# Eight of twelve adaLN parts moved from TensorE to VectorE, as row sums over transposed weight pieces that sit in three of the weight ring's slots

## The chip, the cores and the metric

The kernel runs on one core of one Trainium2 chip. The metric is the device time of one execution, in microseconds (us). Before the change it is 1217.66 us (median of three runs, 1216.58 to 1221.11).

## The reference

Two groups of 128 tokens, a context group and a latent group (256 token columns in all, width 1024), go through two layers of the same form. Each layer first computes a modulation from a condition vector: one fixed vector for the context group, one given vector for the latent group.

```python
mod = silu(cond) @ w_ada + b_ada          # w_ada is 1024 x 6144, per layer
sh1, sc1, g1, sh2, sc2, g2 = split(mod, 6)
h = rms_norm(x, norm1) * (1 + sc1) + sh1
# attention, Hyena and retention branches from h @ w_in, gates from h @ w_gate
x = x + g1 * (merged @ w_out)
h2 = rms_norm(x, norm2) * (1 + sc2) + sh2
x = x + g2 * moe(h2, ...)
```

All is float32. The six parts of `mod` have 1024 values for each of the two condition vectors. Each needs 4 MB of `w_ada`. Two layers of six parts make the twelve parts of the title. A part is named here by layer and number: (0, 2) is `g1` of layer 0; numbers 0 to 5 are sh1, sc1, g1, sh2, sc2, g2.

## The kernel before

**Weights.** SyncE's queue (line 541) fetches all weights in pieces of 1 MB in an order fixed beforehand (`weight_plan`, `ring_table`). The pieces go into a ring of eight slots (`ring`); for the experts six more slots (`lent`) join, once the last merge piece is used. A fetch waits until TensorE has counted off the piece that was in its slot before (`s_weights_used`). The queue is in order: a fetch that waits holds up all fetches behind it.

**A layer, dense half.** TensorE works through units. Units 0 to 29 (`proj`, L747 and L752) are 32 matmuls of 256 columns over one 1 MB piece each. Unit u writes PSUM bank u % 4, and takes it only when the reader of unit u - 4 has freed it. Units 0 to 5 are Hyena's: ScalarE makes the middle tap (L1415), VectorE adds the two other taps and frees the bank (L1660). Behind unit 2, ScalarE and VectorE also make the decay tables of the retention (`decay_tables`, L1394 to L1408 on ScalarE, L1652 to L1660 on VectorE). Units 6 and up are queries, keys, values, gates. Small products stand between the units: Fourier products (L815), retention scores, the eight softmaxes of the attention at units 19 to 27 (scores L891 and L892). Then come six merge pieces (L932) and four output pieces (L961). Each engine's order is written out by hand; engines meet only at semaphores.

**Opening of layer 0** (`first_units_of_first`): units 0 to 3 go in two halves of the depth, with Hyena's filter products (L714 to L728) and part (0, 1) in between.

**The modulation.** All twelve parts are made alike. `ada` (L676) takes four 1 MB pieces and issues 64 matmuls, the condition `condT` as the stationary operand. ScalarE copies the result to `mod_row` (`mod_rows`, L1323), `ada_turn` transposes it with two matmuls (L688), and VectorE adds the bias and makes the factors (`mod_add`). Where each part stands in the order is given by `ADA_AFTER`: (0, 2), (0, 3), (0, 4) behind units 4, 5, 7 of layer 0; (1, 1) and (1, 0) in the merge of layer 0; (1, 2) ahead of unit 0 of layer 1, and (1, 3), (1, 4) behind its units 3 and 5. (0, 0) and (0, 1) stand in the opening, (0, 5) and (1, 5) between the router and the experts.

**Experts half.** 96 pieces of 1 MB per layer, each used once (L1056, L1095, L1071, L1113), with gathers (L1036) and combines (L1136) of tokens in between.

**GpSimd's queue** issues the small loads and stores; in layer 0 the caches are loaded after part (0, 1) is there, and in layer 1 after the last expert piece of layer 0 is used.

Of the kernel before, what the change touches and what calls it, by code (L numbers as in the profile page):

```python
# [17 lines left out]
ALU = mybir.AluOpType  # L18
# [63 lines left out]
def ada_bank(layer, u):  # L82

    return {(0, 5): 5, (0, 7): 7}.get((layer, u), 4)
# [9 lines left out]
def weight_plan():  # L94

    plan = []
    for layer in range(DEPTH):
        if layer == 0:
            plan += OPENING
        for u in range(0 if layer else 3, U_MERGE):  # L100
            beside = [("ada", layer, ADA_AFTER[layer, u])] if (layer, u) in ADA_AFTER else []
            plan += beside + [("proj", layer, u)] if u == 0 else [("proj", layer, u)] + beside
        for m in range(6):
            plan.append(("merge", layer, m))
            if m in (2, 4) and layer + 1 < DEPTH:
                plan.append(("ada", layer + 1, 1 if m == 2 else 0))
# [12 lines left out]
def ring_table():  # L119
# [19 lines left out]
SLOT, FILL, USED = ring_table()  # L139
ADA_ORDER = [item[1:] for item in PLAN if item[0] == "ada"]  # L140


def ada_at(layer, q):

    return ADA_ORDER.index((layer, q))

# [119 lines left out]
def trunk_program(nc, row_scratch, weights, experts, mod_params, params, consts, shared, x_in, k_cache, v_cache, s_cache,  # L266
                  y_out, k_out, v_out, s_out):
    with ExitStack() as ctx:
# [38 lines left out]
        s_b_half = sem("b_half")  # L307
# [7 lines left out]
        s_decay_log = sem("decay_log")  # L315
        s_decay_one = sem("decay_one")
# [12 lines left out]
        s_lam_sums = sem("lam_sums")  # L329
# [17 lines left out]
        s_mod_sum = sem("mod_sum")  # L347
        s_norm_mean = sem("norm_mean")
# [18 lines left out]
        s_scalar_link = sem("scalar_link")  # L367
# [5 lines left out]
        s_stores_read = sem("stores_read")  # L373
        s_taps = sem("taps")
        s_taps_abs = sem("taps_abs")
        s_taps_decayed = sem("taps_decayed")
# [35 lines left out]
        uc = sb("uc", P, 12, TOK)  # L412

# [116 lines left out]
        def _(sp):  # L530
            sp.dma_start(x[:, :, :], x_in).then_inc(s_x_in, 16)
            sp.dma_start(shd[:, :], shared).then_inc(s_shared_in, 16)
            n = dense = 0

# [9 lines left out]
            for kind, layer, _ in PLAN:  # L544
# [6 lines left out]
                sp.wait_ge(s_stores_read, layer + 1)  # L551
# [32 lines left out]
        def _(pool):  # L584
# [15 lines left out]
            for layer in range(DEPTH):  # L600
# [12 lines left out]
                pool.dma_start(sc[:, :, :, :], s_cache[layer]).then_inc(s_cache_in, 16)  # L613
                pool.wait_ge(s_qkr_copied, 2 * layer + 2)
# [16 lines left out]
                pool.sem_inc(s_stores_read, 1)  # L631
# [10 lines left out]
        def _(pe):  # L642
# [49 lines left out]
            def filter_step(layer, n):  # L692
# [30 lines left out]
                else:  # L723
                    pe.wait_ge(s_taps, layer + 1)
# [194 lines left out]
            def merge(layer):  # L919
                u = U_MERGE  # L920
                for half in range(2):
                    for branch, src, event in ((1, uc, s_yb_ready), (2, gr, s_yc_ready),
# [16 lines left out]
                        if (half, branch) == (1, 2):  # L939
                            turn_rows(layer)  # L940
                            if layer + 1 < DEPTH:
                                ada(layer + 1, 0, 4)
                        if layer + 1 < DEPTH and (half, branch) == (1, 0):
                            ada_turn(layer + 1, 0, 4)
                        if layer + 1 < DEPTH and (half, branch) == (0, 0):
                            ada(layer + 1, 1, 4)
                        if layer + 1 < DEPTH and (half, branch) == (1, 1):
                            ada_turn(layer + 1, 1, 4)
# [234 lines left out]
            for layer in range(DEPTH):  # L1183
# [7 lines left out]
                else:  # L1191
                    ada(layer, ADA_AFTER[layer, 0], 4)
                    first_units(layer)
                for u in range(U_MERGE):
                    if u >= (2 if layer else 4):
                        proj(layer, u)
                    if u and (layer, u) in ADA_AFTER:
# [1261 lines left out]
```

## Time and profile before

| | us |
|---|---|
| median of three runs | 1217.66 |
| profiled execution, its own time | 1220.16 |
| span of that execution (first to last instruction) | 1218.4 |
| TensorE matmuls busy in the span | 1171.0 (96%) |
| TensorE weight loads busy | 897.5 (74%) |
| VectorE busy | 359.9 (30%) |
| ScalarE busy | 216.3 (18%) |
| mean granted TensorE clock | 0.986 of full |

All later readings are in us from the start of the span. Layer 0 runs from 0 to about 632, layer 1 from there to the end; in each the experts start about 250 us before its end. The chain of waits is the path followed back from the last instruction. A row of the timeline gives start, duration, engine, line, and in brackets how long the engine sat idle before it and what it waited for. "PEclk" is the granted TensorE clock as a share of full speed (1.00 is 2.4 GHz, 0.50 is 1.2 GHz).

### The profile page before, as it was taken

How to read it: one execution, taken by the hardware profiler on the slowest of the kernel's cores; microseconds unless marked ns; L12 is line 12 of the kernel's file. 1: busy time of each engine (PE TensorE's matmuls, PEld its weight loads, DVE VectorE, ACT ScalarE, POOL GpSimd, SP SyncE). 2: the span in 40 equal slices, each digit the busy share in tenths (PEclk: the TensorE clock that was granted, in tenths of full speed). 3: DMA queues.
4: the chain of work that ended last, by engine and by line, in shares of the span. 5: the costliest groups of instructions: out<-in, count | busy, mean ns of one | idle time of the engine just before them, and what ended most of it. 6: DMA issues, size and time to landing. Idle time of an engine off the chain costs nothing.

```text
span 1218.4 us, 18282 instructions
## 1 busy us (share of the span) xinstructions
PE 1171.0 (96%) x7494; PEld 897.5 (74%) x7494; DVE 359.9 (30%) x905; ACT 216.3 (18%) x459; POOL 39.5 (3%) x80
## 2 busy tenths in 40 slices
PE   6999999999999999989999999999999999998996
PEld 4778888878788775646558888888888877565653
DVE  2541153133326321111233323332242541111113
ACT  2140012232011100111024111132301201000011
POOL 1001110000000000000000012000000000000000
PEclk8999999999998999999999999999999899999998
DMA  9879534333797998999986945343247599899992
GB/s 383 339 284 393 183 130 142 136 112 139 278 408 306 405 401 341 421 421 420 421 331 258 373 153 165 113 147 138 107 155 314 231 391 416 326 423 420 421 420 109
DMA packets 50874, 349.46 MB, mean 287 GB/s; under 512 B 6401, under 2 KB 6561, under 8 KB 9569
## 3 DMA queue, kind: packets, MB, share of 16 engines
q1 hardware_dynamic: 46944, 337.75, 69.7%
q0 software_dynamic: 3840, 10.47, 2.5%
q8 instruction: 62, 1.02, 0.3%
q14 instruction: 28, 0.22, 0.1%
HBM read 343.98 MB, written 2.64 MB: 284 GB/s over the span
## 4 chain that ended last, share of the span: by engine, by line
PE 87%; DMA 8%; DVE 2%; ACT 1%; SPq 1%; issue 1%; DVEq 0%; ACTq 0%
PE bank L752 25%; PE bank L1056 12%; PE bank L1095 7%; PE bank L932 7%; PE bank L961 5%; PE bank L747 5%; PE bank L1036 4%; DMA ring<-in_experts 4%; PE bank L763 4%; PE bank L1136 4%; PE bank L676 4%; DMA lent<-in_experts 3%; DMA ring<-in_weights 1%; PE bank L1071 1%; PE bank L1012 1%; SPq L541 1%
## 5 line engine op out<-in xcount | busy, mean ns | idle before, releaser
L752 PE MATMUL bank<-h,ring 128*128 128x256 f32 x1472 | 326.3, 380 | 0.0
L752 PEld LDWEIGHTS bank<-h,ring 128*128 128x128 f32 x1472 | 276.8, 190 | 40.9 <-issue 4.4
L1056 PE MATMUL bank<-ring,gates 128*64 128x256 f32 (+2 forms) x1280 | 148.7, 379 | 7.1 <-DMA lent<-in_experts 3.5
L1056 PEld LDWEIGHTS bank<-ring,gates 128*64 128x64 f32 (+2 forms) x1280 | 104.3, 137 | 45.4 <-issue 7.5
L1095 PE MATMUL bank<-lent,gates 128*64 128x512 f32 (+2 forms) x288 | 67.0, 637 | 9.5 <-DMA lent<-in_experts 9.5
L1056 PE MATMUL bank<-lent,gates 128*64 128x256 f32 (+1 forms) x640 | 64.7, 380 | 1.4 <-ACT gates L1580 1.4
L1036 PE MATMUL bank<-uc,gates 128*128 128x128 f32 x512 | 60.4, 276 | 0.1
L1036 PEld LDWEIGHTS bank<-uc,gates 128*128 128x128 f32 x512 | 58.6, 192 | 0.7 <-DVE uc L1656 0.4
L932 PE MATMUL bank<-lent,ring 128*128 128x256 f32 x256 | 56.4, 380 | 0.0
L747 PE MATMUL bank<-ring,h 128*128 128x256 f32 x256 | 56.4, 379 | 0.0
L961 PE MATMUL bank<-uc,ring 128*128 128x256 f32 x256 | 55.6, 379 | 0.0
L1056 PEld LDWEIGHTS bank<-lent,gates 128*64 128x64 f32 (+1 forms) x640 | 39.2, 126 | 21.2 <-issue 2.3
L1095 PEld LDWEIGHTS bank<-lent,gates 128*64 128x64 f32 (+2 forms) x288 | 21.3, 141 | 44.9 <-issue 44.9
L932 PEld LDWEIGHTS bank<-lent,ring 128*128 128x128 f32 x256 | 48.4, 190 | 6.9 <-issue 0.4
L961 PEld LDWEIGHTS bank<-uc,ring 128*128 128x128 f32 x256 | 48.6, 190 | 6.6
L1136 PEld LDWEIGHTS bank<-gates,uc 128*128 128x128 f32 x224 | 41.6, 190 | 15.8 <-issue 10.8
L747 PEld LDWEIGHTS bank<-ring,h 128*128 128x128 f32 x256 | 48.1, 190 | 6.2
L1660 DVE SCALAR_TENSOR_TENSOR gates<-gates,bank 128x512 f32<-128x512 f32 (+1 forms) x16 | 10.5, 654 | 141.3 <-issue 108.9
L1136 PE MATMUL bank<-gates,uc 128*128 128x256 f32 x224 | 51.9, 385 | 0.0
L763 PE MATMUL bank<-h,ring 128*128 128x256 f32 x192 | 46.2, 400 | 2.5 <-ACT h L1312 2.5
L2191 DVE COPY uc<-bank 128x512 f32<-128x512 f32 x14 | 9.7, 692 | 130.2 <-PE bank L1095 130.2
L1600 ACT ACTIVATE gates<-bank 128x512 f32<-128x512 f32 (+1 forms) x16 | 9.1, 570 | 212.2 <-PE bank L1056 190.3
(257 smaller groups left out, 1144.8 us busy)
## 6 DMA issues: line engine op xcount, KB each, us to landing
ring<-in_weights SPq DMA_DIRECT2D x128, 1024.0 KB, 5.7
ring<-in_experts SPq DMA_DIRECT2D x108, 1024.0 KB, 20.9
lent<-in_experts SPq DMA_DIRECT2D x84, 1024.0 KB, 16.7
lent<-lent POOLq DMA_DIRECT2D x48, 32.0 KB, 3.2
cst<-in_consts POOLq DMA_DIRECT2D x1, 1345.0 KB, 12.2
x<-in_x_in SPq DMA_DIRECT2D x1, 1024.0 KB, 4.9
lent<-in_s_cache POOLq DMA_DIRECT2D x2, 512.0 KB, 11.5
va<-row_scratch POOLq DMA_DIRECT2D x2, 512.0 KB, 6.7
```

The lines of the kernel that those rows point to most:

```text
L541: sp.dma_start(slot, source).then_inc(s_weights_in[SLOT[n]], 16)
L676: last = pe.matmul(bank[b][32 * j:32 * j + 32, 0:256], condT[:, k, :], w[j][:, k, :], start=(k == 0), stop=(k == KT - 1), skip_group_check ...
L747: last = pe.matmul(bank[b][:, g * 256:(g + 1) * 256], h[:, k, g_cols(g)], w[:, k, :], start=(k == 0), stop=(k == KT - 1))
L752: last = pe.matmul(bank[b][:, c * TOK:(c + 1) * TOK], w[:, k, c * P:(c + 1) * P], h[:, k, :], start=(k == 0), stop=(k == KT - 1))
L763: last = pe.matmul(bank[u][:, c * TOK:(c + 1) * TOK], w[:, k, c * P:(c + 1) * P], h[:, k, :], start=(k == 0 and c == 0), stop=(k == KT - 1 ...
L932: last = pe.matmul(bank[b][:, c * TOK:(c + 1) * TOK], w[:, k, d * P:(d + 1) * P], src[:, k, :], start=(k == 0), stop=(k == 3))
L961: last = pe.matmul(out[c], w[:, k, c * P:(c + 1) * P], merged[:, k, :], start=(k == 0), stop=(k == KT - 1))
L1012: last = pe.matmul(bank[b][:, c * P:(c + 1) * P], h[:, k, g_cols(n // 2)], ident, start=True, stop=True)
L1036: last = pe.matmul(bank[4 + half][:, c * P:(c + 1) * P], htok[:, g, k * P:(k + 1) * P], pick[p % 2][:, g, :], start=(g == 0), stop=(g == 1))
L1056: last = pe.matmul(bank[b][rows, half * 256:half * 256 + 256], hgat[:, k, rows], w[j][:, k, :], start=(k == 0), stop=(k == KT - 1), skip_g ...
L1095: last = pe.matmul(bank[5 - half][rows, :], actT[p % 2][:, f, rows], w[j][:, f, :], start=(f == 0), stop=(f == 3), skip_group_check=True)
L1136: last = pe.matmul(bank[dt // 2][:, (dt % 2) * TOK:(dt % 2 + 1) * TOK], ysb[:, dt * P:(dt + 1) * P], matrix, start=(fresh and dt % 2 == 0) ...
```

## The change

The eight parts (0, 2), (0, 3), (0, 4), (1, 0) to (1, 4) are no longer made by TensorE. `w_ada` for them is laid out transposed, in 64 chunks of 128 output columns by 1024 (512 KB), so that a row sum over a chunk times the condition gives 128 values of `mod`. VectorE does it with one scalar_tensor_tensor with a row sum for each of the two conditions. Parts (0, 0), (0, 1), (0, 5) and (1, 5) stay as they were.

Slots 5, 6 and 7 of the ring hold, through the dense half, the condition rows on all partitions (8 KB each), three landing places for chunks, and a dump for the product. So the dense pieces behind the opening use five slots (`LEAST`), and the experts eight and six as before. The condition rows are loaded raw by GpSimd's queue, once TensorE has used the opening's pieces up to unit 2; ScalarE takes a tanh behind its work on unit 1, VectorE makes the SiLU behind the decay tables, and the rows are stored to memory and loaded again for layer 1. Chunks are fetched by SyncE's queue, each behind a given piece of the plan; VectorE uses them at given places of its order (`HOOKS`, with the count of chunks at each in `AT_HOOK`).

```diff
-ADA_AFTER = {(0, 4): 2, (0, 5): 3, (0, 7): 4, (1, 0): 2, (1, 3): 3, (1, 5): 4}
+LEAST = 5
+MADE = [[(0, 2), (0, 3), (0, 4), (1, 0), (1, 1)], [(1, 2), (1, 3), (1, 4)]]
+CHUNKS = [8 * len(parts) for parts in MADE]
+LANDINGS = 3
+HOOKS = [("conv", 3, 3), ("conv", 4, 4), ("conv", 5, 5), ("rope", 0, 6), ("spectrum", 0, 9),
+         ("decay", 0, 10), ("spectrum", 1, 12), ("hyena", 1, 14), ("gate", 0, 16), ("retain", 1, 17),
+         ("softmax", 0, 18), ("softmax", 1, 19), ("softmax", 2, 20), ("softmax", 3, 21),
+         ("softmax", 4, 22), ("softmax", 5, 24), ("softmax", 7, 26), ("norm", 3, 28),
+         ("merge", 1, 30), ("merge", 3, 32), ("merge", 5, 34), ("merge", 7, 36), ("merge", 9, 38)]
+AT_HOOK = [[1, 1, 1, 6, 1, 3, 5, 1, 1, 2, 1, 1, 1, 1, 4, 1, 1, 4, 1, 1, 1, 1, 0],
+           [1, 1, 1, 5, 1, 3, 4, 1, 1, 2, 0, 1, 1, 1, 1, 0, 0, 0, 0, 0, 0, 0, 0]]
+def chunks_behind():
...
+            for c in range(count):
+                at = unit + 2 + c // LANDINGS
+                item = ("proj", layer, at) if at < U_MERGE else ("merge", layer, (at - U_MERGE) // 2)
+                behind.setdefault(item, []).append(n)
+                n += 1
...
-        since = {at: free[at] for at in range(SLOTS)}
+        own = SLOTS if kind == "moe" or (kind, layer, _) in OPENING else LEAST
+        since = {at: free[at] for at in range(own)}
...
+        cond_wide = ring[:, LEAST, :].rearrange("p (c k) -> p c k", c=2)
+        landing = [ring[:, LEAST + 1 + n // 2, D * (n % 2):D * (n % 2) + D] for n in range(LANDINGS)]
+        raw = ring[:, LEAST + 1, :]
+        product = ring[:, SLOTS - 1, D:2 * D]
...
+            def fetch_chunk():
+                nonlocal chunk
+                n = chunk % LANDINGS
+                if chunk == 0:
+                    sp.wait_ge(s_cond_ready, 2)
+                elif chunk == CHUNKS[0]:
+                    sp.wait_ge(s_weights_used, END["moe", 0, 0])
+                if chunk >= LANDINGS:
+                    sp.wait_ge(s_chunk_used, chunk - LANDINGS + 1)
+                sp.dma_start(landing[n], mod_weights[chunk, :, :]).then_inc(s_chunk_in[n], 16)
+                chunk += 1
...
                         fetch(weights[dense, :, :])
                         dense += 1
+                    for _ in CHUNKS_BEHIND.get((kind, layer, number), ()):
+                        fetch_chunk()
                     continue
...
+                sp.wait_ge(s_chunk_used, sum(CHUNKS[:layer + 1]))
...
                 if layer == 0:
+                    pool.wait_ge(s_weights_used, END["ada", 0, 1])
+                    pool.wait_ge(s_weights_used, MADE_FREE)
+                    pool.dma_start(raw, cond_rows.broadcast_to([P, 2 * D])).then_inc(s_cond_moved, 16)
                     pool.wait_ge(s_mod_ready, ada_at(0, 1) + 1)
...
                     pool.wait_ge(s_weights_used, END["moe", layer - 1, 0])
+                    pool.dma_start(flat(cond_wide), cond_scratch.broadcast_to([P, 2 * D])).then_inc(
+                        s_cond_moved, 16)
...
-                    ada(layer, ADA_AFTER[layer, 0], 4)
...
-                    if (layer, u) in ADA_AFTER:
-                        mod_rows(layer, ADA_AFTER[layer, u], ada_bank(layer, u))
+                    if layer == 0 and u == 1:
+                        sc_e.wait_ge(s_cond_moved, 16)
+                        sc_e.activation(flat(cond_wide), raw, ACT.Tanh, scale=0.5).then_inc(
+                            s_cond_tanh, 1)
...
+            def make_parts(layer, hook, number):
...
+                        dve.wait_ge(s_chunk_in[n % LANDINGS], 16 * (n // LANDINGS + 1))
...
+                        if n:
+                            dve.wait_ge(s_chunk_used, n)
+                        w = landing[n % LANDINGS]
+                        for c, out in enumerate((product, w)):
+                            last = dve.scalar_tensor_tensor(
+                                out, w, 0.5, cond_wide[:, c, :], ALU.mult, ALU.mult,
+                                accum_out=mod_all[:, of, row, c:c + 1])
+                        last.then_inc(s_chunk_used, 1)
+                        if n % 8 == 7:
+                            dve.wait_ge(s_chunk_used, n + 1)
+                            part_finish(of, q)
...
                     if u == 2:
                         decay_tables()
+                        if layer == 0:
+                            dve.wait_ge(s_cond_tanh, 2)
+                            stt(flat(cond_wide), flat(cond_wide), 1.0, raw, ALU.add, ALU.mult).then_inc(
+                                s_cond_ready, 1)
+                            dve.wait_ge(s_cond_ready, 2)
+                    make_parts(layer, "conv", u)
```

`MADE_FREE` is the count of `s_weights_used` at the end of unit 2 of layer 0. The calls of `ada`, `ada_turn`, `mod_rows` and `mod_add` for the eight parts are gone everywhere, also in the merge of layer 0. `part_finish` adds the bias and makes the factors (one or two small VectorE instructions per part). Calls of `make_parts` stand at the places that `HOOKS` names: ahead of a rotary step, a spectrum, a decay or a softmax, and behind a merge half-unit. A few semaphores that counted one event each are joined into one, with the same waits; ScalarE's waits on stores now read the stores' own semaphore.

## Rows read from the trace of the kernel before

**Rows 1.** The page, part 1: busy us, share of the span, instructions.

```profile
PE 1171.0 (96%) x7494; PEld 897.5 (74%) x7494; DVE 359.9 (30%) x905; ACT 216.3 (18%) x459; POOL 39.5 (3%) x80
```

**Rows 2.** Waits of TensorE, whole span: us in total, times, longest.

```profile
PE bank L1095 <- DMA lent<-in_experts: 9.5, 2, 4.9
```

**Rows 3.** The chain in order of time: start us, us, what.

```profile
69.82 6.91 PE bank L752 x32
76.72 3.59 PE bank L676 x64
...
683.38 3.59 PE bank L676 x64
```

**Rows 4.** Timeline of layer 0, a transpose between two units.

```profile
98.12 0.38 PE L688 MATMUL bank<-cst,rinv 128*128 128x128 f32 x2
...
98.34 7.07 PE L752 MATMUL bank<-h,ring 128*128 128x256 f32 x32
```

**Rows 5.** Timeline, start of layer 1.

```profile
633.00 3.66 PE L676 MATMUL bank<-ring,condT 128*32 128x256 f32 x64 [0.67 <-DVEq L1666]
...
635.75 0.49 ACT L1312 ACTIVATE h<-h,modT,amp 128x128 f32<-128x128 f32 x1 [2.35 <-DVE h L1652]
...
636.59 14.08 PE L763 MATMUL bank<-h,ring 128*128 128x256 f32 x64
...
651.57 13.98 PE L752 MATMUL bank<-h,ring 128*128 128x256 f32 x64
```

**Rows 6.** Windows of the opening: us, PE, PEld, DVE, ACT, POOL busy, PEclk, DMA share, GB/s.

```profile
21.60:25.10 3.50, 0.41 (x3) 0.23 (x3) 1.92 (x8) 0.88 (x2) 0.00 (x0) 0.88 1.02 421
25.10:28.50 3.40, 3.40 (x8) 2.74 (x9) 1.71 (x5) 2.76 (x4) 0.00 (x0) 0.50 1.00 419
28.50:31.70 3.20, 3.20 (x10) 2.27 (x9) 0.00 (x0) 0.00 (x0) 0.00 (x0) 0.60 1.02 424
```

**Rows 7.** Timeline of layer 0, units 2 and 3 and the decay tables.

```profile
62.75 7.07 PE L763 MATMUL bank<-h,ring 128*128 128x256 f32 x32
...
66.40 1.02 ACT L1415 ACTIVATE uc<-bank,par 128x256 f32<-128x256 f32 x2 [7.58 <-PE bank L763]
...
79.19 0.69 DVE L1652 TENSOR_TENSOR dsum<-dsum,lent 128x512 f32<-128x512 f32 x1
```

**Rows 8.** DMA issues: KB each, median us from issue to landing.

```profile
ring<-in_weights SPq DMA_DIRECT2D x128, 1024.0 KB, 5.7
...
cst<-in_consts POOLq DMA_DIRECT2D x1, 1345.0 KB, 12.2
...
va<-row_scratch POOLq DMA_DIRECT2D x2, 512.0 KB, 6.7
```

**Rows 9.** ScalarE's groups by shape: busy us, mean ns, idle before.

```profile
L1478 ACT ACTIVATION_READ_ACCUMULATOR lent<-bank,sm 128x1 f32 x32 | 6.3, 197 | 0.0
...
L1334 ACT ACTIVATE vr<-va 128x1024 f32<-128x1024 f32 x2 | 2.1, 1057 | 9.4 <-DVEq L1718 9.3
```

**Rows 10.** VectorE's groups by shape, same columns.

```profile
L1660 DVE SCALAR_TENSOR_TENSOR lent<-rinv,lent 128x512 f32<-128x512 f32 x4 | 2.8, 692 | 0.6
...
L1652 DVE TENSOR_TENSOR uc<-uc 128x1024 f32<-128x1024 f32 x2 | 2.5, 1226 | 0.3
```

**Rows 11.** Timeline of VectorE in layer 0, first work of softmaxes 1 and 4.

```profile
217.40 0.62 DVE L1910 TENSOR_REDUCE sm<-bank 128x1 f32<-128x128 f32 x2 [4.65 <-PE bank L892]
...
248.08 0.89 DVE L1910 TENSOR_REDUCE sm<-bank 128x1 f32<-128x256 f32 x2 [12.40 <-PE bank L892]
```

**Rows 12.** Windows of the two dense halves, columns as in group 6.

```profile
90.00:341.00 251.00, 249.79 (x1392) 209.94 (x1385) 77.38 (x147) 44.75 (x101) 16.14 (x31) 1.00 0.53 195
674.00:840.00 166.00, 166.00 (x872) 140.90 (x871) 47.66 (x93) 29.30 (x63) 14.54 (x28) 1.00 0.50 179
```

**Rows 13.** Timeline of SyncE's queue: first fetches of expert pieces.

```profile
341.62 3.07 SPq L541 DMA_DIRECT2D lent<-in_experts  x6
```

**Rows 14.** A window of the experts half of layer 0, columns as in group 6.

```profile
460.00:473.00 13.00, 13.00 (x118) 7.03 (x118) 2.32 (x9) 0.60 (x1) 0.00 (x0) 1.00 0.76 303
```

More of the change, by code:

```diff
@@ L74 @@
 ADA_PIECES = 4
-ADA_AFTER = {(0, 4): 2, (0, 5): 3, (0, 7): 4, (1, 0): 2, (1, 3): 3, (1, 5): 4}
+LEAST = 5
[9 more added lines that the diff above has]
+           [1, 1, 1, 5, 1, 3, 4, 1, 1, 2, 0, 1, 1, 1, 1, 0, 0, 0, 0, 0, 0, 0, 0]]
+assert [sum(n) for n in AT_HOOK] == CHUNKS
+def chunks_behind():
+    behind = {}
+    for layer in range(DEPTH):
+        n = 0
+        for (_, _, unit), count in zip(HOOKS, AT_HOOK[layer]):
+            for c in range(count):
[3 more added lines that the diff above has]
+                n += 1
+    return behind
 OPENING = [("ada", 0, 0), ("proj", 0, 0), ("proj", 0, 1), ("proj", 0, 2), ("ada", 0, 1)]
 OPENING_DONE = [("ada", 0, 0), ("ada", 0, 1), ("proj", 0, 0), ("proj", 0, 1), ("proj", 0, 2)]
-def ada_bank(layer, u):
-    return {(0, 5): 5, (0, 7): 7}.get((layer, u), 4)
 def ada_parts(layer, q):
@@ L100, in weight_plan @@
         for u in range(0 if layer else 3, U_MERGE):
-            beside = [("ada", layer, ADA_AFTER[layer, u])] if (layer, u) in ADA_AFTER else []
-            plan += beside + [("proj", layer, u)] if u == 0 else [("proj", layer, u)] + beside
+            plan.append(("proj", layer, u))
         for m in range(6):
             plan.append(("merge", layer, m))
-            if m in (2, 4) and layer + 1 < DEPTH:
-                plan.append(("ada", layer + 1, 1 if m == 2 else 0))
         plan += [("out", layer, u) for u in range(U_OUT, N_PROJ)]
@@ L145, in ada_at, with made_at @@
     return ADA_ORDER.index((layer, q))
+def made_at(layer, q):
+    return [part for parts in MADE for part in parts].index((layer, q)) + 1
 def proj_end(layer, u):
@@ L347, in trunk_program @@
         s_mod_sum = sem("mod_sum")
+        s_chunk_in = [sem(f"chunk_in{n}") for n in range(LANDINGS)]
+        s_chunk_used = sem("chunk_used")
+        s_part_made = sem("part_made")
+        s_cond_moved = sem("cond_rows_in_out_in")
         s_norm_mean = sem("norm_mean")
@@ L542, in fetch @@
                 n += 1
-            for kind, layer, _ in PLAN:
+            for kind, layer, number in PLAN:
                 if kind != "moe":
@@ L1308, in norm_shift @@
                 else:
-                    sc_e.wait_ge(s_mod_ready, 1 + max(ada_at(layer, q) for q in range(2)))
+                    sc_e.wait_ge(s_part_made, made_at(layer, 1))
                 for k in tiles_:
@@ L1709, in mod_add @@
                 if q == 2:
-                    link(ts(modT[:, 16:24, :], modT[:, 16:24, :], 0.5, ALU.mult))
-                dve.sem_inc(s_mod_ready, 1)
+                    link(ts(mine, mine, 0.5, ALU.mult))
+                dve.sem_inc(s_part_made, 1)
+            def make_parts(layer, hook, number):
+                for (name, which, _), count in zip(HOOKS, AT_HOOK[layer]):
+                    if (name, which) != (hook, number):
+                        continue
+                    for _ in range(count):
+                        n = made[0]
+                        made[0] += 1
+                        of, q = MADE[layer][(n - sum(CHUNKS[:layer])) // 8]
+                        row = 8 * q + n % 8
+                        dve.wait_ge(s_chunk_in[n % LANDINGS], 16 * (n // LANDINGS + 1))
+                        if n == CHUNKS[0]:
+                            dve.wait_ge(s_cond_moved, 48)
+                        if n:
[9 more added lines that the diff above has]
+                            part_finish(of, q)
             def taps_decay(layer):
@@ L1930, in _ @@
                 dve.sem_inc(s_qx_ready, 1)
+                make_parts(layer, "spectrum", 0)
                 spectrum(0)
+                make_parts(layer, "decay", 0)
                 ret_decay(0)
+                make_parts(layer, "spectrum", 1)
                 spectrum(1)
@@ L1946, in _ @@
                         ret_decay(1)
+                make_parts(layer, "gate", 0)
                 yc_gate(0)
@@ L1958, in _ @@
                 for i in range(8):
+                    make_parts(layer, "softmax", i)
                     if i == 5:
@@ L1964, in _ @@
                         ya(0)
+                make_parts(layer, "norm", 3)
                 o_mean(3)
@@ L1996, in _ @@
                                 dve.sem_inc(s_merged, 1)
+                            make_parts(layer, "merge", u - U_MERGE)
                             u += 1
-                        if layer + 1 < DEPTH and (half, n) == (1, 0):
-                            mod_add(layer + 1, 1, 4)
-                        if layer + 1 < DEPTH and (half, n) == (1, 2):
-                            mod_add(layer + 1, 0, 4)
                 def square_add(t):
@@ L2383, in lay_out @@
     weights = np.stack(pieces)
+    mod_weights = np.stack([a["w_ada"][l][:, D * q + P * t:D * q + P * t + P].T
+                            for parts in MADE for l, q in parts for t in range(KT)])
+    cond_rows = np.concatenate([a["c_ctx"].reshape(-1), a["c"][0].reshape(-1)])[None]
     experts = np.stack([np.stack([
```

95 lines of the change are left out of this document (39 added, 56 removed).

## The prediction

> **What bounds the kernel now.** I read the shares first. TensorE is busy 96% of the span and VectorE 30% [rows 1]. So work that leaves TensorE is worth its time, where nothing else then ends last. The waits of TensorE say where that could be: its largest is for expert weights, 9.5 us in two waits [rows 2], so the experts half is nearly paced by DMA and the dense half is not. The chain agrees. In the dense half it is unit behind unit, 6.91 us each, and the parts stand in it in full, 3.59 us each; of those removed it holds seven at that length, from the one at 76.72 to the one at 683.38 [rows 3]. The chain shows no cover for them.
>
> **What goes.** Seven parts stand between other work: 7 x 3.59 = 25.1 us. Each has its transposes too: a unit ends at 98.12, the next starts at 98.34 [rows 4], 0.22 us, seven times 1.5 us. The eighth, (1, 2), runs at 633.00 while layer 1's norm is made. The first h tile is ready at 635.75 + 0.49 = 636.24 and units 0 and 1 start at 636.59, so removing it brings 0.35 us there. Their 64 matmuls last 2 x 6.91 = 13.8 us, to 650.4, and unit 2 starts at 651.57 [rows 5]: 1.1 us for that part's transposes and their wait for ScalarE's copy go as well. In all 25.1 + 1.5 + 1.5 = 28.1 us. Most of it lies in stages where every gap is full, so I take it whole; the least would be 25.1 alone.
>
> **The hole at the start of layer 1.** Without (1, 2) TensorE sits idle from the end of the norm's sum, 633.00 - 0.67 = 632.3 [rows 5], to about 636.3. The opening shows such a pause: 0.41 us of work in 3.5 us, and then the granted clock is 0.50 for 3.4 us and 0.60 on average for 3.2 us [rows 6]. That is 3.4 + 2.6 = 6.0 us at the lower of the two levels, 1.2 GHz, which loses half of it, 3.0 us. I take 3.0 us, from 0 (the clock holds) to 3.4.
>
> **The hole in layer 0, the largest cost.** Chunk 0 stands in SyncE's queue behind the piece of unit 5, and its fetch waits for the condition rows in their final form. The pieces of units 6 and up stand behind it; they were fetched freely before. Step by step:
> - Unit 2 is over at 66.3 (half of the row at 62.75) and ScalarE starts on it at 66.40 [rows 7]. Only then may GpSimd's queue load the raw rows, 1 MB on its software queue. The trace has 512 KB there in 6.7 us (a broadcast of the same kind) and 1345 KB in 12.2 us, the latter beside a full DMA; on SyncE's queue 1 MB takes 5.7 us [rows 8]. DMA is free at this point, since SyncE's queue waits, so I take 6.0 us: 72.4.
> - ScalarE waits for them behind unit 1's tap, ahead of unit 2's. Then the tanh over 2048 columns, twice the 1057 ns for 1024 [rows 9]: 2.1 us, to 74.5. So unit 2's tap, at 66.40 before, is 8.1 us late.
> - All that hangs on it moves by as much: the decay tables end at 79.19 + 0.69 = 79.9 before [rows 7], now at 88.0.
> - VectorE's SiLU over 2048 columns, twice 1226 ns [rows 10]: 90.4.
> - SyncE's queue issues chunk 0, then unit 6's piece (0.3 us), 5.7 us to land [rows 8], and half a megabyte is ahead of it, about 0.6 us at half of a landing's excess: 97.0.
> - TensorE does units 4 and 5 from 69.8, and would start unit 6 at 69.8 + 2 x 6.91 = 83.6. It waits until 97.0: 13.4 us. After such a hole I charge the low clock again, 3.0 us.
>
> The bounds: with the raw rows there at once, the decay tables still end at 79.9 and the piece lands at 88.9, a hole of 5.3 us and perhaps no loss of clock. With 12.2 us for the rows and 8.5 us for the piece it is 22.4 us and 3.0 for the clock. I take 16.4 us, from 5.3 to 25.4, near the middle because the uncontended rows are the nearest. The Trainium skill (DMA: Bandwidth & Descriptors, Anatomy of one DMA) fits a GpSimd DMA by a fixed 2.0 us plus its bytes at 436 GB/s, 4.4 us for this one by estimate; the sum would be 1.6 us lower by it. No row has a lone 1 MB on that queue.
>
> **What is added on VectorE.** A chunk is two instructions over 1024 columns. The trace has none with a row sum. The plain two-input instruction over 1024 takes 1226 ns, and scalar_tensor_tensor over two SBUF inputs takes the same as it at 512 columns, 692 ns [rows 10]. ScalarE's reading of a row sum is an instruction of its own, 197 ns [rows 9]. So a chunk is 2.45 us at least and 2.85 with that reading; I take 2.7, and 64 make 173 us. The other end is double, 4.9 us, a rival below. VectorE has 174 us of nothing to do from 90 to 341 and 118 from 674 to 840 [rows 12], for 40 x 2.7 = 108 and 24 x 2.7 = 65 us. What decides is each place. One chunk ahead of a softmax fits in 4.65 us of idle time, four ahead of the fifth (10.8 us) in 12.40 us [rows 11]. Six stand ahead of the rotary step; its result is wanted only at unit 16. So I put chunks at nothing, as long as one costs under 12.40 / 4 = 3.1 us.
>
> **Moved fetches.** Each chunk's fetch waits for the chunk three before it, and holds the pieces behind. With five slots a piece is asked for five units ahead, so it has 35 us; the worst hold, at the rotary step (six chunks), ends about 12 us before unit 10 wants its piece. Nothing. Layer 1's condition rows are loaded at its start and first used behind unit 3: hidden. In the experts half the fetches began at 341.62, when the last merge piece was used [rows 13]. Now the fourth piece of part (0, 5) waits for a slot that output unit 44 gives back, 20.7 us later, and nine expert pieces stand behind it. At 421 GB/s [rows 6] a piece takes 2.5 us, so the ten are there by 341.6 + 20.7 + 25 = 387.3, ahead of the first expert matmul at 391. The next are asked for when the first are used, as before, by a DMA about 4 us behind. It has room: 0.76 share in 460 to 473, 3.1 us idle [rows 14], while no piece is wanted. I take 0, at most 4 us for each layer.
>
> **The sum.** -28.1 + 13.4 + 3.0 + 3.0 = -8.7 us. Of the profiled execution's 1220.16 us that leaves 1211.5. It lay 2.5 us above the median of the runs, so I predict 1209.0 us. About 0.5% (6 us) is what a measurement can tell from no change.
>
> **Rivals.**
> - *The hole eats the gain.* The raw rows take 10 us or more, or SyncE's queue is held again later by chunks. For: contended landings of 12.2 us. Against: DMA is empty there. Hole and clock 22 to 25 us: 1215 to 1218, no change that can be measured. Chance 0.20.
> - *VectorE becomes the bound (slower).* The row sum makes the instruction run at half rate: 2 x 2.25 + 0.4 = 4.9 us a chunk. From 90.4 on VectorE then has 40 x 4.9 + 77.4 [rows 12] = 273 us in layer 0 and ends at 364, where the merge would end at 338 (341 - 19.2 + 16.4): 26 us late, and some 10 more since it also waits for TensorE in order. Layer 1: 118 + 47.7 = 165 us in a stretch of 155, 10 us, and 4 for the clock. 1209 + 50 = 1259 us. It decides from 3.1 us a chunk. Against it: plain two-input instructions run at one column per 1.04 ns. The Trainium skill (Vector Engine (DVE) Microarchitecture Reference, Points that are easy to get wrong) says just this: a scalar_tensor_tensor with two SBUF sources that are not bf16 has half the throughput, no port being left for the accumulator. By the trace such an instruction without a row sum is not slowed (692 ns for 512 columns); with one, no row shows it. Chance 0.14.
> - *Little of a hole.* The rows land in 4 us or less and the clock holds: hole 9 us, no clock loss, 1220.16 - 28.1 + 9 - 2.5 = 1198.6. Against: the decay tables alone end too late for unit 6. Chance 0.08.
> - *It doesn't spare TensorE's time*, since parts were cover for something late. For: (1, 2) was such cover. Against: the seven others stand between full units. Within the same 1215 and up; counted in the first rival.
>
> **Chances.** The forecast with a hole of 9 to 20 us, 1202 to 1214, has 0.58. Faster by over 0.5% (under 1211.6) takes most of it, 0.54, and all of the third rival: 0.62. Within 0.5%: 0.04 and the first rival's 0.20 less a little: 0.23. Slower: 0.14 and a rest: 0.15. The range is 1199 to 1222; below lies a shorter hole, above it VectorE as the bound.
>
> **What would show it.** TensorE waits for the piece of unit 6 from about 84 to 97 in the chain, with DMA and SyncE's queue in it; the decay tables end at 88; clock at 0.5 behind both holes; of the twelve groups of 64 matmuls at L676 four are left; chunk instructions near 1.3 us; the stretch from unit 7 to the last merge piece without a wait for VectorE. Wrong would be: unit 6 at 84, chunks over 3 us each, or new DMA waits in the experts half.

## Result and the profile after

The changed kernel takes 1208.64 us (median of five runs, 1206.81 to 1209.46) against 1217.66: a ratio of 0.9917, with a 95% interval of 0.9903 to 0.9931. The forecast was 1209.0. The profiled execution of the changed kernel has a span of 1207.7 us against 1218.4, at a mean granted clock of 0.978.

The page of the kernel after: busy time and share of each engine [against rows 1], then TensorE's clock in 40 slices.

```profile
PE 1144.6 (95%) x6966; PEld 883.0 (73%) x6966; DVE 510.8 (42%) x1154; ACT 215.3 (18%) x452; POOL 41.2 (3%) x83
```

```profile
PEclk9998999999998999989999999999999899998999
```

TensorE has 26.4 us less to do and VectorE 150.9 us more, and the span is only 10.7 us shorter. The largest waits of TensorE (engine, line, what it waited for: total, times, longest) say where the rest is [against rows 2]:

```profile
PE bank L806 <- DMA ring<-in_weights: 13.1, 1, 13.1
PE bank L1141 <- DMA lent<-in_experts: 9.5, 2, 4.9
PE bank L790 <- ACT h L1332: 6.9, 1, 6.9
PE bank L817 <- ACT h L1346: 6.6, 2, 4.0
PE bank L1102 <- DMA ring<-in_experts: 4.8, 3, 2.5
```

The first is new, and is the hole in layer 0. The second is unchanged, and so, but for 0.1 us, is the third, the first norm of the opening. Of the fourth 4.0 us is new, the start of layer 1. No wait for a chunk or a made part is in the list.

The hole, in the timeline (start, duration, engine, line; idle time before it in brackets), one fence for each engine. GpSimd's queue, ScalarE:

```profile
66.20 0.53 POOL L655 DMA_DIRECT2D ring<-in_cond_rows  x1 [47.55 <-PE bank L817]
```

```profile
72.40 1.91 ACT L1454 ACTIVATE ring<-ring 128x2048 f32<-128x2048 f32 x1 [13.01 <-DMA ring<-in_cond_rows]
74.21 1.00 ACT L1449 ACTIVATE uc<-bank,par 128x256 f32<-128x256 f32 x2
```

VectorE, the last of the decay tables and the product over the condition rows; SyncE's queue, chunk 0 and unit 6's piece; TensorE, unit 6:

```profile
86.98 0.69 DVE L1682 TENSOR_TENSOR dsum<-dsum,lent 128x512 f32<-128x512 f32 x1
87.71 2.29 DVE L1690 SCALAR_TENSOR_TENSOR ring<-ring 128x2048 f32<-128x2048 f32 x1
```

```profile
90.03 0.33 SPq L575 DMA_DIRECT2D ring<-in_mod_weights  x1
90.40 0.43 SPq L584 DMA_DIRECT2D ring<-in_weights  x1
```

```profile
95.99 4.63 PE L806 MATMUL bank<-h,ring 128*128 128x256 f32 x10 [13.09 <-DMA ring<-in_weights]
```

Every step of the prediction is there, in its order: rows at 72.4, tables at 87.7, product at 90.0, piece at 96.0. The windows (busy time of each engine, then PEclk, DMA share and GB/s) of the hole, of the 7 us behind it, and of the start of layer 1 show the clock:

```profile
83.00:96.00 13.00, 0.01 (x1) 0.01 (x1) 8.88 (x13) 5.21 (x16) 0.51 (x1) 0.66 0.38 143
96.00:103.00 7.00, 7.00 (x22) 5.79 (x23) 6.34 (x13) 0.00 (x0) 0.00 (x0) 0.66 1.01 424
632.80:637.00 4.20, 4.17 (x12) 3.41 (x13) 3.98 (x13) 2.96 (x6) 0.00 (x0) 0.59 0.00 0
```

A granted clock of 0.66 in the mean is a mix of the two levels, 1.2 and 2.4 GHz. The 64 matmuls behind the hole last 16.4 us instead of 13.8, a loss of 2.6. Layer 1's start, in the timeline:

```profile
625.16 3.62 PE L790 MATMUL bank<-h,ones 128*128 128x256 f32 x16
632.83 15.74 PE L817 MATMUL bank<-h,ring 128*128 128x256 f32 x64 [4.05 <-ACT h L1346]
648.40 11.82 PE L806 MATMUL bank<-h,ring 128*128 128x256 f32 x54
```

Here 64 matmuls last 15.7 us, 1.9 more than at full clock. From the norm's sum to unit 2 it was 651.57 - 628.72 = 22.85 us before and is 648.40 - 625.16 = 23.24 now: taking part (1, 2) away brought nothing there, the stretch is even 0.4 us longer.

The chunks, in the groups by line (busy time, mean ns | idle before) [against rows 9 and 10]:

```profile
L1770 DVE SCALAR_TENSOR_TENSOR ring<-ring 128x1024 f32<-128x1024 f32 x128 | 151.7, 1223 | 17.5 <-DMA ring<-in_mod_weights 8.9 <-DVE lent L1682 2.6 <-DVE uc L1690 1.9
L1770 DVE DVE_READ_ACCUMULATOR ring<-ring 128x1 f32 x128 | 10.7, 83 | 0.0
```

Stage by stage, from starts in the two timelines, before to after: the opening to unit 3, 69.82 to 69.09 (-0.7; its first weights landed 0.7 us earlier; in the kernels below unit 3 starts 0.3 us earlier to 2.7 us later than here, so I count this as scatter and not as the change); from there to the output projection, 271.2 to 267.0 us (-4.2: five parts out, the hole in); to the first expert matmul, 45.7 both; layer 0's experts 242.05 to 243.39 (+1.3); layer 1's start +0.4; its dense half 319.0 to 311.0 (-8.0: two parts); its experts +0.4. The sum is -10.8.

### The profile page after: what moved, and what is told of

Read it like the earlier page. It is cut to its first block, busy times and chain, and to the rows that moved or that the text cites. A ratio compares the mean times of both kernels' runs of the same rounds, so it can differ in the third digit from the quotient of the medians.

```text
span 1207.7 us, 17513 instructions
## 1 busy us (share of the span) xinstructions
PE 1144.6 (95%) x6966; PEld 883.0 (73%) x6966; DVE 510.8 (42%) x1154; ACT 215.3 (18%) x452; POOL 41.2 (3%) x83
## 4 chain that ended last, share of the span: by engine, by line
PE 83%; DMA 11%; DVE 3%; ACT 2%; issue 1%; SPq 1%; DVEq 0%; ACTq 0%; POOLq 0%
PE bank L806 24%; PE bank L1102 12%; PE bank L1141 7%; PE bank L986 7%; PE bank L1007 5%; PE bank L801 5%; PE bank L1082 4%; PE bank L1182 4%; DMA lent<-in_experts 4%; DMA ring<-in_experts 4%; DMA ring<-in_weights 3%; PE bank L817 2%; PE bank L730 1%; PE bank L1117 1%; PE bank L1058 1%
## 5 line engine op out<-in xcount | busy, mean ns | idle before, releaser
L806 PE MATMUL bank<-h,ring 128*128 128x256 f32 x1472 | 327.4, 382 | 13.1 <-DMA ring<-in_weights 13.1
L1770 DVE SCALAR_TENSOR_TENSOR ring<-ring 128x1024 f32<-128x1024 f32 x128 | 151.7, 1223 | 17.5 <-DMA ring<-in_mod_weights 8.9
L1102 PE MATMUL bank<-lent,gates 128*64 128x256 f32 (+2 forms) x896 | 127.0, 380 | 2.3 <-ACT gates L1610 2.3
L1102 PE MATMUL bank<-ring,gates 128*64 128x256 f32 (+2 forms) x1024 | 121.0, 380 | 6.2 <-DMA ring<-in_experts 4.8
L1102 PEld LDWEIGHTS bank<-lent,gates 128*64 128x64 f32 (+2 forms) x896 | 82.6, 137 | 36.3 <-ACT gates L1610 2.8
L1141 PE MATMUL bank<-ring,gates 128*64 128x512 f32 (+2 forms) x304 | 83.7, 613 | 9.5 <-DMA lent<-in_experts 9.5
L1141 PE MATMUL bank<-lent,gates 128*64 128x512 f32 (+2 forms) x176 | 55.0, 688 | 0.0
L1182 PEld LDWEIGHTS bank<-gates,uc 128*128 128x128 f32 x224 | 41.6, 190 | 15.9 <-issue 10.8
## 6 DMA issues: line engine op xcount, KB each, us to landing
ring<-in_experts SPq DMA_DIRECT2D x108, 1024.0 KB, 21.2
lent<-in_experts SPq DMA_DIRECT2D x84, 1024.0 KB, 19.9
```

What stands on the lines that cost most here:

```text
L806: last = pe.matmul(bank[b][:, c * TOK:(c + 1) * TOK], w[:, k, c * P:(c + 1) * P], h[:, k, :], start=(k == 0), stop=(k == KT - 1))
L1102: last = pe.matmul(bank[b][rows, half * 256:half * 256 + 256], hgat[:, k, rows], w[j][:, k, :], start=(k == 0), stop=(k == KT - 1), skip_g ...
L1141: last = pe.matmul(bank[5 - half][rows, :], actT[p % 2][:, f, rows], w[j][:, f, :], start=(f == 0), stop=(f == 3), skip_group_check=True)
L1182: last = pe.matmul(bank[dt // 2][:, (dt % 2) * TOK:(dt % 2 + 1) * TOK], ysb[:, dt * P:(dt + 1) * P], matrix, start=(fresh and dt % 2 == 0) ...
L1770: last = dve.scalar_tensor_tensor(out, w, 0.5, cond_wide[:, c, :], ALU.mult, ALU.mult, accum_out=mod_all[:, of, row, c:c + 1])
```

## Experiments

All times are medians; ratios are against the kernel before, measured beside each of them (1217.4 to 1217.8 us).

**Is the hole the queue's order?** In layer 0 no chunk is fetched ahead of the piece of unit 8:

```diff
-AT_HOOK = [[1, 1, 1, 6, 1, 3, 5, 1, 1, 2, 1, 1, 1, 1, 4, 1, 1, 4, 1, 1, 1, 1, 0],
+AT_HOOK = [[0, 0, 0, 6, 2, 3, 5, 1, 2, 2, 1, 1, 1, 1, 4, 1, 1, 4, 1, 1, 1, 1, 1],
```

> The changed kernel with one table edited: in layer 0 no chunk is fetched before the piece of unit 8; the three chunks that stood behind units 3, 4 and 5 are spread over three later hooks. SyncE's queue then fetches the pieces of units 6, 7 and 8 freely, as before the change. The raw rows, the tanh, the decay tables and the SiLU stay where they are. Theory A (the hole in front of unit 6, 13.1 us, and the low clock behind it, 2.6 us, are nothing but the queue's order): no DMA wait in front of unit 6, 15.7 us won. The late decay tables then show: VectorE reaches unit 3's tap only at about 90 and gives bank 3 back at about 92, and TensorE wants it for unit 7 at 83.0 + 6.9 = 89.9, a wait of some 2 us. Sum 1208.6 - 15.7 + 2 = 1195. Rival B (VectorE has no room for three more chunks later on): TensorE waits for VectorE at softmax or merge, 5 us or more of the gain given back, 1200 and up. Rival C (the late decay tables alone make the hole, since banks come free late): a wait for VectorE of 8 us or more near 84 to 95, 1203 or more.

1195.26 us, ratio 0.982 (0.9802 to 0.9838): 13.4 us under the changed kernel. Theory A. Its waits have no DMA in front of unit 6, and one new row, the late bank:

```profile
PE bank L806 <- DVEq L1883: 1.1, 1, 1.1
```

**Are the late taps a cost of their own?** As above, and the condition rows are finished behind unit 5:

```diff
-                    if layer == 0 and u == 1:
+                    if layer == 0 and u == 5:
                         sc_e.wait_ge(s_cond_moved, 16)
...
                     if u == 2:
                         decay_tables()
-                        if layer == 0:
-                            dve.wait_ge(s_cond_tanh, 2)
+                    if layer == 0 and u == 5:
+                        dve.wait_ge(s_cond_tanh, 2)
```

> As the kernel with later chunks, and in layer 0 ScalarE's tanh over the condition rows stands behind its tap of unit 5 instead of unit 1, and VectorE's SiLU product behind its tap of unit 5 instead of behind the decay tables of unit 2. The taps of unit 2 no longer wait for the raw rows, so the decay tables should end near 80 us instead of 87.7. Theory A: the wait for bank 3 in front of unit 7 is gone, TensorE runs without a gap from the opening to unit 12, 1193 us (2 us under the kernel with later chunks). The SiLU ends at about 86 to 90, the first chunk is asked for behind unit 8's piece at once, and unit 9's piece lands before 97, wanted at 104. Rival: VectorE's start on the chunks becomes later than the SP queue can bear, and a unit behind 8 waits for its piece: a DMA wait of some us at 104 to 120, 1196 or more. If the late tap never mattered once the queue is free, it equals the kernel with later chunks within 0.5 us.

1192.76 us, ratio 0.9791 (0.9777 to 0.9806). TensorE runs on through unit 7 without a gap:

```profile
74.82 21.96 PE L806 MATMUL bank<-h,ring 128*128 128x256 f32 x101
```

The 1.1 us wait is gone. The intervals of this kernel and of the one with later chunks overlap a little, so what the trace shows, 1.1 us, is the surer size.

**Which step in front of the product made it late?** Only the order on VectorE is changed, the chunks stay:

```diff
                     if u == 2:
-                        decay_tables()
                         if layer == 0:
...
                             dve.wait_ge(s_cond_ready, 2)
+                        decay_tables()
```

> The changed kernel with two steps of VectorE in layer 0 exchanged: the SiLU product over the condition rows stands ahead of the decay tables of unit 2 and not behind them. The chunks keep their places, so chunk 0 still stands in SyncE's queue ahead of the piece of unit 6. Theory A (the decay tables in front of the product are what made the hole long, the raw rows are only its first part): the tanh ends at 74.3 and unit 2's taps at about 76, the product at 78.5, chunk 0 is asked for at 78.5, unit 6's piece at 78.9 and lands at about 84.5, 1.5 us after it is wanted instead of 13.1; the clock holds; the decay tables end at 90 and bank 3 comes free for unit 7 about 1 us late. 1208.6 - 11.6 - 2.6 + 1 = 1195.4. Rival (the queue is held by something else as well, such as GpSimd's loads of the caches): a hole of 5 us or more, 1199 and up.

1201.39 us, ratio 0.9862 (0.9847 to 0.9877): 7.3 us won, not 13. The hole shrank to 2.9 us, where I expected 1.5 (VectorE's taps of unit 2 ended at 77.4 and the product at 79.9, each 1.4 us later than I worked out), and the 64 matmuls behind it last 14.1 us, so there is no loss of clock. But beside this wait there is a new one, the first of these two:

```profile
PE bank L862 <- DVEq L1893: 5.1, 1, 5.1
PE bank L806 <- DMA ring<-in_weights: 2.9, 1, 2.9
```

Now the taps of units 3 to 5, with a chunk behind each, end too late for the first transpose of Hyena's product (L862), and the 64 matmuls behind this wait last 15.4 us instead of 14.0, so the clock is lost here instead. In the changed kernel the 13.1 us hole had hidden this. It is not the late tables alone: in the kernel with later chunks the taps start about as late (88.6 us, here 90.1), but without the three chunks between them the product is ready at 96.5 instead of 104.9, and L862 does not wait. So the order on VectorE made the hole long, as expected, and what the hole had hidden behind it are tables and chunks together.

**Does idle time cost the clock?** Idle matmuls of ones in both holes (their results are not used):

```diff
+                    spin(2, 15)
                     first_units(layer)
...
+                    if (layer, u) == (0, 6):
+                        spin(6, 54)
```

> The changed kernel, with idle matmuls of ones in two holes: 54 in front of unit 6 of layer 0 (some 12.4 us by the opening's 0.23 us each) and 15 between layer 1's norm sum and its unit 0 (3.4 us). The holes stay as long as they are. Their results are not used. Theory A (the idle time itself lowers the granted clock behind it): clock 1.0 behind both, 64 matmuls at 13.8 us instead of 16.4 and 15.7; 1208.6 - 2.6 - 1.9 = 1204.1. Rival B (the clock falls for another reason, say the load of the DMA or of VectorE at that moment): the same 16.4 and 15.7, 1208.6. Rival C (the idle matmuls themselves end late): a fraction of a us lost, over 1205.

1204.84 us, ratio 0.9896 (0.9881 to 0.9911), 3.8 us under the changed kernel, 4.5 expected. Both holes are filled, and the groups behind them run at full speed:

```profile
83.11 12.22 PE L719 MATMUL bank<-ones 128*128 128x128 f32 x108
96.46 14.08 PE L806 MATMUL bank<-h,ring 128*128 128x256 f32 x64 [1.13 <-DMA ring<-in_weights]
```

```profile
625.98 3.51 PE L719 MATMUL bank<-ones 128*128 128x128 f32 x30
630.20 14.05 PE L817 MATMUL bank<-h,ring 128*128 128x256 f32 x64 [0.71 <-ACT h L1349]
```

**How near is VectorE?** Every row sum computed twice (c over both conditions, ahead of the old pair), and in a second kernel one of the two sums only:

```diff
+                        for c in range(2):
+                            link(dve.scalar_tensor_tensor(
+                                product, w, 0.5, cond_wide[:, c, :], ALU.mult, ALU.mult,
+                                accum_out=mod_all[:, of, row, c:c + 1]))
                         for c, out in enumerate((product, w)):
```

> The changed kernel with each chunk's two row sums computed twice, so that a chunk costs VectorE about 5.1 us instead of 2.48 (4 x 1.22 and two more reads and waits). This is the price at which the rival of the prediction had VectorE as the bound. Theory A (that rival's sum): from 90 on VectorE has 40 x 5.1 + 77.4 = 281 us of work in layer 0 and ends at 371 where the merge ends at 336, 35 us late and some 10 for waits in order; layer 1 has 24 x 5.1 + 47.7 = 170 us in 155, 15 us, and 4 for the clock: 1208.6 + 64 = 1273, in any case over 1250. TensorE would show long waits for VectorE and DMA-held pieces. Rival B (VectorE's slack lies where the chunks stand, and TensorE waits for it little): under 1225.

1305.46 us, ratio 1.0711 (1.069 to 1.0732): 96.8 us more, worse than the 64 of the rival's sum. Its first waits:

```profile
PE bank L902 <- DVEq L1918: 30.0, 2, 17.0
PE bank L806 <- DMA ring<-in_weights: 18.3, 4, 11.7
PE bank L876 <- DVEq L1941: 10.5, 2, 6.1
```

> The changed kernel with the first row sum of every chunk computed twice, so that a chunk costs VectorE about 3.8 us instead of 2.48. The prediction put the point from which chunks cost TensorE time at 3.1 us. Theory A (what decides is each place: the row of the doubled sums showed 30 us of waits for the second spectrum product and the product before it, where 11 to 18 chunks stand in a row): waits for VectorE's spectrum product of 4 us or so in each layer and some for softmax, 1214 to 1228. Rival B (what decides is the stretch's sum: 90 + 40 x 3.8 + 77.4 = 319 against a merge that ends at 336): within 3 us of 1208.6. Rival C (proportional to the added VectorE time, 96.8 us for 64 x 2.6): 64 x 1.3 = 83 us added, 1257.

1230.3 us, ratio 1.0094 (1.0073 to 1.0114): 21.7 us more for 1.27 us more a chunk. That is nearest to theory A, but 2 us beyond its range; rivals B and C fell. The waits for VectorE of its layer 0, 95 to 400 us, and the unit behind the first:

```profile
PE bank L902 <- DVEq L1917: 12.0, 1, 12.0
PE bank L955 <- DVEq L1947: 2.7, 1, 2.7
```

```profile
179.89 8.92 PE L801 MATMUL bank<-ring,h 128*128 128x256 f32 x32
```

L902 (the first product of the retention) waits for bank 6, which VectorE's second spectrum product gives back, behind 18 chunks. I took this to be a tight place, and moved the five (four) chunks in front of it behind it, in the kernel with three sums:

```diff
-AT_HOOK = [[1, 1, 1, 6, 1, 3, 5, 1, 1, 2, 1, 1, 1, 1, 4, 1, 1, 4, 1, 1, 1, 1, 0],
-           [1, 1, 1, 5, 1, 3, 4, 1, 1, 2, 0, 1, 1, 1, 1, 0, 0, 0, 0, 0, 0, 0, 0]]
+AT_HOOK = [[1, 1, 1, 6, 1, 3, 0, 3, 3, 3, 1, 1, 1, 1, 4, 1, 1, 4, 1, 1, 1, 1, 0],
+           [1, 1, 1, 5, 1, 3, 0, 3, 2, 2, 0, 1, 1, 1, 1, 1, 0, 0, 0, 0, 0, 0, 0]]
```

> The kernel with three sums a chunk (3.75 us a chunk), and the five (layer 1: four) chunks that stand ahead of VectorE's second spectrum product are moved behind it. With the chunks at their old places that kernel took 1230.3 us, with waits of 12.0 and 4.4 us of TensorE for bank 6, which that product gives back. Theory A (the place decides: the margin was 3.7 us at bank 6, and nowhere else so small): both waits for bank 6 vanish, and 12.0 + 4.4 + 2.3 for the clock are won, less some new wait at the gates and the softmax: 1212 to 1218. Rival B (VectorE is full over the whole stretch, the wait only moves to the next place): 1226 and up.

1231.84 us, ratio 1.0121 (1.0104 to 1.0137), so nothing was won. Theory A fell. The 12.0 us at bank 6 are gone, and most of their length is back at later places of layer 0:

```profile
PE bank L946 <- ACTq L1538: 6.4, 1, 6.4
PE bank L923 <- DVEq L2029: 3.3, 1, 3.3
PE bank L955 <- DVEq L1947: 1.4, 1, 1.4
```

The longest is at the first softmax's scores, and the unit behind it runs slow:

```profile
226.89 1.41 PE L946 MATMUL bank<-lent 64*128 64x128 f32 x4 [6.43 <-ACTq L1538]
228.23 9.93 PE L806 MATMUL bank<-h,ring 128*128 128x256 f32 x32
```

This wait is for ScalarE, which had itself waited for VectorE (21.2 us, to 223.5). So VectorE was full over the whole stretch up to the first softmax, and not at one place. The sum says the same: in the changed kernel it is busy 94.3 us of the 121 from 92 to 213, with 23 chunks, and 23 x 1.27 = 29 us more do not fit. Chunks moved behind the first softmax were not tried.

**Does the smaller ring cost by itself?** The kernel before, all parts on TensorE, dense weights in five slots:

```diff
-        since = {at: free[at] for at in range(SLOTS)}
+        own = SLOTS if kind == "moe" or (kind, layer, _) in OPENING else 5
+        since = {at: free[at] for at in range(own)}
```

> The kernel before the change, with one edit: the weights of the dense half may lie in five of the ring's eight slots only (the opening and the experts keep all eight), as in the changed kernel. All twelve parts stay on TensorE. Theory A (the smaller ring costs nothing in the dense half, as the prediction put it, and a little in the experts half, where SyncE's queue now starts on expert weights some 20 us later): 1217.7 + 1.5 = 1219, with the 1.5 us between layer 0's first expert matmul and layer 1's norm sum. Rival B (it costs nothing anywhere, and the 1.5 us in the changed kernel come from something else): 1217.7. Rival C (a part needs four pieces at once out of five, so each part waits for its last pieces): DMA waits in front of the parts, 5 us or more, 1223 and up; the changed kernel would not have these.

1243.94 us, ratio 1.0214 (1.0194 to 1.0234): rival C, 26 us slower. A part takes four of the five slots at once:

```profile
80.66 7.17 PE L753 MATMUL bank<-h,ring 128*128 128x256 f32 x32 [1.34 <-DMA ring<-in_weights]
91.88 1.51 PE L677 MATMUL bank<-ring,condT 128*32 128x256 f32 x12 [4.04 <-DMA ring<-in_weights]
```

By the starts, layer 0's dense half grew by 13.3 us, layer 1's by 8.4, the experts by 0.9 and 0.2: the 22.8 us by which its span is longer. So lending three slots costs little in the dense half only because these parts no longer go through the ring.

**A version that beats both.** The kernel with late rows, with 15 idle matmuls at the start of layer 1; then also the last part's pieces in all eight slots:

```diff
-        own = SLOTS if kind == "moe" or (kind, layer, _) in OPENING else LEAST
+        own = SLOTS if kind == "moe" or _ == 5 and kind == "ada" or (kind, layer, _) in OPENING else LEAST
...
+                    if (kind, number) == ("ada", 5):
+                        sp.wait_ge(s_chunk_used, sum(CHUNKS[:layer + 1]))
```

> The kernel with late rows (chunks from unit 8 on, tanh and SiLU behind unit 5), and 15 idle matmuls between layer 1's norm sum and its unit 0. Theory A (the clock's loss in layer 1 is independent of the rest): 1192.8 - 2 = 1190.8. Rival: nothing, since the time is given back at a later wait: 1192.8.

> The kernel with late rows and idle matmuls at the start of layer 1, and the four pieces of the last adaLN part of each layer may lie in all eight slots: SyncE's queue waits for the last chunk to be used before it fetches them. Its queue then reaches the first expert weights when the merge is over (about 321 us) instead of 341.7. Theory A (the late start of the expert fetches costs the 1.5 us in layer 0's experts and 0.4 in layer 1's): 1190.8 - 2 = 1189. Rival B (the first waits for expert weights come far later and are set by the rate of the DMA and not by its start): within 0.5 us of the kernel without this edit. Rival C (the wait for the last chunk holds the queue): slower by 1 us or more.

1190.97 us (0.9771, 0.9751 to 0.9791) and 1188.5 us (0.9759, 0.9739 to 0.9779). The second is the fastest found, 29 us under the kernel before. The intervals of neighbouring kernels overlap (late rows, with idle matmuls, with eight slots), so neither step of 2 us is clear of noise by its time. The traces of the last two differ by 1.5 us in layer 0's experts, where SyncE's queue asks for the first expert weights at 320.6 instead of 343.5. The window of 60 us with most of that difference, without and with the eight slots:

```profile
430.00:490.00 60.00, 57.16 (x509) 37.07 (x510) 9.89 (x30) 7.83 (x12) 0.00 (x0) 0.97 1.01 421
```

```profile
429.30:489.30 60.00, 58.36 (x537) 38.08 (x537) 10.52 (x31) 8.43 (x13) 0.00 (x0) 1.00 0.91 365
```

The DMA has caught up (0.91 instead of 1.01), TensorE waits 1.2 us less and keeps its clock.

## Why the prediction was right

Against its terms, in the order of the sum:

- *What goes*, -28.1: held, 1.3 us too low. Five parts are 19.9 us of layer 0 (-4.2 with the 15.7 of the hole and its clock taken out, so this size is what is left over and not measured by itself), two are 8.0 of layer 1, and the start of layer 1 came out at +0.4, which is -1.5 and 1.9 for the clock: 29.4 in all.
- *The hole in layer 0*, +13.4 and +3.0: measured 13.1 and 2.6. The raw rows took 6.2 us from issue to landing (6.0 taken), the tables ended at 87.7 (88.0), the piece landed at 96.0 (97.0). Moving the chunks behind unit 8 won 13.4 us. That the rows came within 0.2 us of what was taken is partly luck: in the nine other kernels that load them the same load took 4.5 to 6.2 us. The Trainium skill's fit for such a DMA (DMA: Bandwidth & Descriptors, Anatomy of one DMA), 4.4 us by estimate, lay 1.8 us under this trace and 0.1 under the shortest; three more loads of that queue stood behind this one each time, so no trace shows it alone.
- *The start of layer 1*, +3.0: 1.9. Of the terms not taken at nothing it was the most off in its share. The opening's pause was too dear a model: there the clock stayed low for 3.4 + 2.6 = 6.0 us [rows 6], here a loss of 1.9 us means some 3.8. With idle matmuls the loss was gone.
- *Chunks at nothing*: held. 2.48 us from chunk to chunk against 2.7 taken. The rival of VectorE as the bound hung on the row sum's rate: 1223 ns for 1024 columns with the sum, 1226 for the plain two-input instruction without [rows 10]. The rule of the Trainium skill (Vector Engine (DVE) Microarchitecture Reference, Points that are easy to get wrong) gives a scalar_tensor_tensor with two SBUF sources that are not bf16 half the throughput. The prediction took this as half the rate of a plain two-input instruction, and read so it does not hold here. Against an instruction with one SBUF source the kernel before does show a half, and without any row sum:

```profile
L1656 DVE TENSOR_SCALAR lent<-lent,sm 128x256 f32<-128x256 f32 x8 | 2.8, 353 | 0.3
L1656 DVE TENSOR_SCALAR lent<-lent,sm 128x128 f32<-128x128 f32 x8 | 2.3, 286 | 0.3
L1660 DVE SCALAR_TENSOR_TENSOR lent<-lent,sm 128x256 f32<-128x256 f32 x8 | 3.9, 484 | 0.3
L1660 DVE SCALAR_TENSOR_TENSOR lent<-lent,sm 128x128 f32<-128x128 f32 x8 | 2.8, 351 | 0.3
```

  128 more columns cost 67 ns with one source and 133 ns with two. The 1.04 ns a column that the prediction took for the plain two-input instruction is already this half, and the row sum adds nothing to it.
- *The point from which VectorE decides*, 3.1 us a chunk: about right in its number, but from the wrong row. I named one softmax slot and the sum over 250 us; the stretch that fills up lies between, up to the first softmax. There VectorE was busy 59.79 us of the 73 from 92 to 165:

```profile
92.00:165.00 73.00, 69.01 (x317) 58.81 (x318) 59.79 (x104) 5.98 (x10) 12.89 (x25) 0.94 0.91 335
```

  In the kernel with three sums bank 6 came 14.1 us later (177.8 against 163.8) for 18 x 1.27 = 22.9 us of added work, so 8.8 us went into gaps, and TensorE wants the bank 3.8 us after it is free (167.5). (8.8 + 3.8) / 18 = 0.7 us a chunk more, an estimate of 3.2 us. The price beyond it I had too low: at 5.1 us a chunk the rival's sum gives 64 us, and 96.8 was measured.
- *Moved fetches and experts*, 0, at most 4 us a layer: 1.3 and 0.4 us. Five slots are enough for the units, as reasoned, but would have cost 26 us with the parts still in them, which the prediction did not say. In the experts the term that it put at nothing measured 1.7 us; the late start of the expert fetches is its likely cause, since eight slots for part (0, 5) took 1.5 us off layer 0's experts in the trace.

With the terms as measured, -29.4 + 13.1 + 2.6 + 1.9 + 1.7 = -10.1, and 0.7 of scatter in the opening, against -8.7 forecast (the sum closes by itself, since what went was taken from it); the two spans differ by 10.7, the two medians by 9.0. So the last microsecond of agreement is luck (one execution and the median of several differ by as much), and the start of layer 1, 1.1 too dear, and the experts, 1.7 too cheap, cancel in part. The hole and the parts are not luck, but for the landing of the rows.

Open: what sets the loss of clock. The hole of 13.1 us costs only 0.7 us more than the one of 4.0, and in the kernel with the moved chunks the unit behind 6.4 us of waiting loses 2.9 us, more than behind 13.1. And in the kernel with the product first I did not try the taps without the chunks between them; the kernel with later chunks is the nearest to it.

## What to carry to other kernels

When work moves to an idle engine, look for the first thing it needs, and at what stands behind that in an in-order DMA queue: here one wait for 1 MB of condition rows held back weights that had nothing to do with it, and took more than half of the gain. Place the first fetch where its condition is long met. When you judge the room on the receiving engine, look at the stretch up to the next hand-over as a whole as well as at each place: here moving chunks inside it moved the wait and won nothing.

## What the runs showed of the hardware

- A row sum in VectorE's two-input instruction costs no rate: 1223 ns for 1024 float32 columns, and 1226 for the plain two-input instruction without one [rows 10]; reading it out is an instruction of 83 ns, against ScalarE's 197 [rows 9].
- A hole of 2.9 us in TensorE's work left the clock at full (64 matmuls 14.1 us behind it); 4.0 us lost 1.9, 13.1 us lost 2.6, and each loss was gone when idle matmuls filled the hole up to its last microsecond.
- Waits for VectorE or ScalarE cost clock as well as waits for DMA: behind 12.0 us at bank 6 a unit lasts 8.9 us instead of 7.1, behind 6.4 us at the first softmax 9.9, and behind 5.1 us at the first transpose two units last 15.4 instead of 14.0. Among these holes the loss does not go by their length.
- One and the same load of 1 MB on GpSimd's queue took 4.5 to 6.2 us in ten kernels.
